# Seven block products instead of eight for three pieces of the first down projection

## What is computed

```python
def swiglu(h, w_gate, w_up, w_down):                     # first block, inner width 2816
    return (jax.nn.silu(h @ w_gate) * (h @ w_up)) @ w_down
...
x = x + swiglu(rmsnorm(x, norm_ffn), w_ffn_gate, w_ffn_up, w_ffn_down)
return rmsnorm(x, norm_final)                             # and then the second block's norm
...
h = h + jnp.square(jax.nn.relu(u @ w_ff1)) @ w_ff2        # second block, inner width 4096
```

## Time and profile before

| | |
|---|---|
| time, median of 3 runs | 928.12 us (928.05 to 928.24) |
| time of the profiled execution | 928.59 us |
| its span in the trace | 926.8 us |
| TensorE busy (PE) | 912.8 us, 98% |
| VectorE busy (DVE) | 661.6 us, 71% |
| ScalarE busy (ACT) | 500.9 us, 54% |
| GpSimd busy (POOL) | 90.1 us, 10% |
| mean granted TensorE clock | 0.998 |

### The profile page before, as it was taken

The page is one execution under the profiler, slowest core; times in us unless marked ns, Lnnn a source line. Parts: engine busy times, 40 slices in busy tenths (PEclk is TensorE's granted clock), DMA queues, the critical chain, the costliest instruction groups (busy, mean ns, idle before and its releaser), DMA issues.

```text
span 926.8 us, 15782 instructions
## 1 busy us (share of the span) xinstructions
PE 912.8 (98%) x6399; PEld 782.2 (84%) x6399; DVE 661.6 (71%) x1075; ACT 500.9 (54%) x786; POOL 90.1 (10%) x103
## 2 busy tenths in 40 slices
PE   9999999999999999999999999999999999999998
PEld 8999987787778788888888889988988788888886
DVE  5786446556777768777744769578867578888886
ACT  5654345556864456555544674546436455565551
POOL 1000000131004200000000000003350003330000
PEclk9999999999999999999999999999999999999999
DMA  9769842244446435555543442231000445455631
GB/s 326 300 131 275 320 182 91 92 182 136 182 195 252 184 114 204 199 199 195 184 182 119 182 162 92 91 105 80 3 2 21 164 182 182 182 192 197 226 112 46
DMA packets 16872, 149.80 MB, mean 162 GB/s; under 512 B 1744, under 2 KB 6224, under 8 KB 8352
## 3 DMA queue, kind: packets, MB, share of 16 engines
q1 hardware_dynamic: 14688, 140.24, 40.9%
q0 software_dynamic: 1296, 5.24, 3.2%
q10 hardware_dynamic: 816, 3.31, 0.9%
HBM read 144.59 MB, written 4.19 MB: 161 GB/s over the span
## 4 chain that ended last, share of the span: by engine, by line
PE 89%; DVE 4%; ACT 3%; issue 2%; POOL 1%; DMA 0%; ACTq 0%; DVEq 0%; POOLq 0%
PE bank L743 46%; PE bank L785 15%; PE bank L787 7%; PE bank L700 4%; PE bank L1577 3%; PE bank L950 1%; POOL HN L3382 1%; PE bank L987 1%; PE bank L1024 1%; DVE W_LOW L2423 1%; PE bank L861 1%; ACT W_HIGH L1811 1%; PE bank L1444 1%; DMA PRM<-params_dram 0%; PE bank L1338 0%
## 5 line engine op out<-in xcount | busy, mean ns | idle before, releaser
L2423 DVE TENSOR_TENSOR W_LOW<-weights,W_HIGH 128x2048 fp32r<-128x2048 f32 (+1 forms) x98 | 222.4, 2270 | 106.5 <-ACT W_HIGH L1811 105.4
L1811 ACT ACTIVATE W_HIGH<-weights 128x2048 fp32r<-128x2048 f32 (+1 forms) x98 | 184.0, 1878 | 138.4 <-PE bank L743 137.2
L785 PE MATMUL bank<-OVER_BOTH,W_HIGH 128*128 128x512 f32 x608 | 211.6, 392 | 0.2 <-DVE W_LOW L2423 0.2
L787 PE MATMUL bank<-OVER_BOTH,W_LOW 128*128 128x256 f32 x608 | 170.0, 280 | 0.0
L785 PEld LDWEIGHTS bank<-OVER_BOTH,W_HIGH 128*128 128x128 f32 x608 | 114.1, 188 | 25.9 <-DVE W_LOW L2423 0.5
L787 PEld LDWEIGHTS bank<-OVER_BOTH,W_LOW 128*128 128x128 f32 x608 | 114.2, 188 | 0.0
L1749 ACT ACTIVATE ARENA<-bank 128x256 f32<-128x256 f32 x76 | 29.1, 384 | 84.0 <-PE bank L787 83.2
L743 PE MATMUL bank<-W_HIGH,HID_HIGH 128*128 128x512 f32 x164 | 64.0, 390 | 0.0
L743 PE MATMUL bank<-W_HIGH,HID_LOW 128*128 128x512 f32 x164 | 63.9, 390 | 0.0
L743 PE MATMUL bank<-W_LOW,HID_HIGH 128*128 128x512 f32 x164 | 63.9, 390 | 0.0
L743 PE MATMUL bank<-FIRST_HIGH,W_HIGH 128*128 128x256 f32 x216 | 61.5, 285 | 0.0
(11 more groups left out here) (577 smaller groups left out, 1956.2 us busy)
## 6 DMA issues: line engine op xcount, KB each, us to landing
weights<-weights_dram SPq DMA_DIRECT2D x62, 2048.0 KB, 7.9
weights<-weights_dram SPq DMA_DIRECT2D x3, 1024.0 KB, 9.3
bias_rows_dram<-ARENA POOLq DMA_DIRECT2D x1, 3072.0 KB, 39.4
BIAS<-params_dram ACTq DMA_DIRECT2D x1, 1997.0 KB, 14.0
weights<-weights_dram SPq DMA_DIRECT2D x1, 1664.0 KB, 6.5
weights<-weights_dram SPq DMA_DIRECT2D x1, 1584.0 KB, 8.1
weights<-weights_dram SPq DMA_DIRECT2D x3, 512.0 KB, 5.8
X<-x_dram ACTq DMA_DIRECT2D x2, 512.0 KB, 4.2
```

The source lines that it names most:

```text
L785: pe.matmul(o[:, :].rearrange("p (q n) -> p q n", q=2), high, OVER_BOTH[:, :, k, :], start=(k == 0), stop=False, skip_group_check=True)
L787: ins = pe.matmul(o[:, 0:S], low, OVER_HT[:, k, :], start=False, stop=(k == KD - 1), skip_group_check=True)
L1811: act.activation(part_of(like_source(piece_parts(k)[0], k), k), part_of(piece_source(k), k), ACT.Copy)\
L2423: dve.tensor_tensor(low, part_of(src, k), high.bitcast(F32), ALU.subtract)\
```

## The change

Three things are changed. (1) `SEVEN` gets the pieces 2, 4 and 6 of `down1`: they are computed with seven products, with the same operations around them as in `down2`. GpSimd's sums of hidden blocks and their splits lie in the first hidden layer (`ffn1`). (2) The extra banks of `down1` are added to X by a function `extras` in two steps that stand in VectorE's program inside the loop over the pieces: step 0 behind the split of piece 8 (the ninth), step 1 behind the split of piece 9 (the tenth). ScalarE's copy of bank 0 stands behind its split of piece 8. In `down2` both steps stay behind all splits. (3) TensorE waits for `x_gained` before the keep-running matmuls after `down1`, since these write banks 0 to 3.

```diff
-SEVEN = (2, 4, 6, 8, 10, 12)
+SEVEN = [("down1", c) for c in (2, 4, 6)] + [("down2", c) for c in (2, 4, 6, 8, 10, 12)]
...
-        W_SUMS_AT = [0, 0, 1, 0, 1, 0]
+        W_SUMS_AT = [0, 0, 1, 0, 0, 2, 0, 2, 0]
...
         def wait_sums_place(eng, n):
-            if n == 0:
-                eng.wait_ge(sem("jobs_written"), len(JOBS))
-            elif n == W_SUMS_AT.index(1):
-                eng.wait_ge(sem("down2_pieces_read"), 4)
+            kind = SEVEN[n][0]
+            before = [SEVEN[m][1] for m in range(n) if SEVEN[m][0] == kind and W_SUMS_AT[m] == W_SUMS_AT[n]]
+            if before:
+                eng.wait_ge(sem(kind + "_pieces_read"), before[-1] + 1)
+            elif W_SUMS_AT[n]:
+                eng.wait_ge(sem(kind + "_pieces_read"), 4)
             else:
-                last = max(m for m in range(n) if W_SUMS_AT[m] == W_SUMS_AT[n])
-                eng.wait_ge(sem("down2_pieces_read"), SEVEN[last] + 1)
+                eng.wait_ge(sem("jobs_written"), max(k for job, k in JOB_AT.items() if job[0] == "ffn" + kind[-1]) + 1)
...
                 for c in range(nk // 2 - 2):
-                    if kind == "down2" and c in SEVEN:
+                    if (kind, c) in SEVEN:
                         ready(2 * c + 1)
-                        ins = seven_products(c, high, low)
+                        ins = seven_products(kind, c, high, low)
...
+            pe.wait_ge(sem("x_gained"), 1)
             norm_transposes(2, (4, 3, 2))
...
             def hidden1_high(c):
+                if ("down1", c - 1) in SEVEN:
+                    hidden_sums_high(SEVEN.index(("down1", c - 1)))
                 act.wait_ge(sem("hidden_ready"), c + 1)
...
-            for k in range(PIECE_AT["down1", 0, 0] + 2, in2 + 1):
+            down1 = PIECE_AT["down1", 0, 0]
+            for k in range(down1 + 2, in2 + 1):
                 split_high(k)
+                if k == down1 + last_of("down1") + 2:
+                    act.wait_ge(sem("down1_pieces_read"), last_of("down1") + 1)
+                    act.activation(EXTRA1[:, 0, :], BK[0][:, :], ACT.Copy).then_inc(sem("cross_by_act"), 1)
...
+            def extras(kind, sums, scales, copied, step):
+
+                def gain(tt, dc, src):
+                    xs = X[:, tt, dc * 512:(dc + 1) * 512]
+                    return dve.scalar_tensor_tensor(out=xs, in0=src, scalar=scales[:, tt:tt + 1], in1=xs, op0=ALU.mult, op1=ALU.add)
+
+                if step == 0:
+                    dve.wait_ge(sem(kind + "_pieces_read"), last_of(kind) + 1)
+                    dve.wait_ge(sem("cross_by_act"), copied)
+                    link(dve.tensor_tensor(sums[:, 1, :], BK[2][:, :], sums[:, 0, :], ALU.add))
+                    gain(0, 0, sums[:, 0, :])
+                    link(gain(0, 1, sums[:, 1, :]))
+                    link(dve.tensor_tensor(sums[:, 0, :], BK[3][:, :], sums[:, 1, :], ALU.add))
+                else:
+                    gain(0, 1, BK[1][:, :])
+                    gain(1, 0, sums[:, 0, :])
+                    link(gain(1, 1, sums[:, 0, :]))
+                    link(gain(1, 1, BK[1][:, :]))
...
             def hidden1_low(c):
+                if ("down1", c - 1) in SEVEN:
+                    hidden_sums_low(SEVEN.index(("down1", c - 1)))
                 hidden_low(HID1_HIGH, HID1_LOW, slice(2 * c, 2 * c + 2), HF1[:, c % 2, :], c)
...
                 if c >= 2 and t == 0:
                     dve.wait_ge(sem("hidden_split" if j else "hidden_ready"), c - 1)
+                    if j and ("down1", c - 2) in SEVEN:
+                        dve.wait_ge(sem("hidden_sums"), 3 * SEVEN.index(("down1", c - 2)) + 3)
...
-            for k in range(PIECE_AT["down1", 0, 0] + 2, in2 + 1):
+            down1 = PIECE_AT["down1", 0, 0]
+            for k in range(down1 + 2, in2 + 1):
                 split_low(k)
+                if k - down1 - last_of("down1") in (2, 3):
+                    extras("down1", EXTRA1, HALF_RSTD, 4 * FF1_CHUNKS + 1, k - down1 - last_of("down1") - 2)
```

More of the change, by code:

```diff
@@ L493, in seven @@
             kind, i, j = PIECES[k]
-            return SEVEN.index(2 * i + j) if kind == "down2" and 2 * i + j in SEVEN else None
+            return SEVEN.index((kind, 2 * i + j)) if (kind, 2 * i + j) in SEVEN else None
         def part_of(t, k):
@@ L1115, in _, with seven_products @@
                 branch_product(i)
[L1118 to L1122, removed]
+            def seven_products(kind, c, high, low):
+                n = SEVEN.index((kind, c))
+                w, hid, sums = split_piece(kind, c // 2, c % 2), HID_SUMS[n], W_SUMS[W_SUMS_AT[n]]
+                opens, closes = n == first_of(kind), c == last_of(kind)
+                if opens:
                     for b in range(4):
-                        pe.wait_ge(sem(f"job_out{b}"), len(range(b, len(JOBS), 4)))
+                        pe.wait_ge(sem(f"job_out{b}"), len(range(b, state["job"], 4)))
                 def product(o, left, right, own):
                     return product3(o[:, :], [[part] for part in left], [[part] for part in right],
-                                    first=own and n == 0, last=own and n == len(SEVEN) - 1)
+                                    first=own and opens, last=own and closes)
                 def hidden(t, k):
@@ L2352, in _ @@
             act.wait_ge(sem("hidden_split"), FF1_CHUNKS + FF2_KT // 2)
-            act.wait_ge(sem("down2_pieces_read"), SEVEN[-1] + 1)
+            act.wait_ge(sem("down2_pieces_read"), last_of("down2") + 1)
             act.activation(HF2[:, 0, :], BK[0][:, :], ACT.Copy).then_inc(sem("cross_by_act"), 1)
@@ L3272, in _ @@
             link(dve.reciprocal(RSTD, SUMSQ))
[L3274 to L3278, removed]
             def hidden2_low(q):
-                if q - 1 in SEVEN:
-                    hidden_sums_low(SEVEN.index(q - 1))
+                if ("down2", q - 1) in SEVEN:
+                    hidden_sums_low(SEVEN.index(("down2", q - 1)))
                 hidden_low(HID2_HIGH, HID2_LOW, slice(2 * q, 2 * q + 2), HF2[:, q % 2, :], FF1_CHUNKS + q)
@@ L3304, in _ @@
                 split_low(k)
-            def gain(tt, dc, src):
-                xs = X[:, tt, dc * 512:(dc + 1) * 512]
-                return dve.scalar_tensor_tensor(out=xs, in0=src, scalar=RSTD[:, tt:tt + 1], in1=xs, op0=ALU.mult, op1=ALU.add)
-            dve.wait_ge(sem("down2_pieces_read"), SEVEN[-1] + 1)
-            dve.wait_ge(sem("cross_by_act"), 4 * (FF1_CHUNKS + FF2_CHUNKS) + 1)
-            link(dve.tensor_tensor(HF2[:, 1, :], BK[2][:, :], HF2[:, 0, :], ALU.add))
-            gain(0, 0, HF2[:, 0, :])
-            link(gain(0, 1, HF2[:, 1, :]))
-            link(dve.tensor_tensor(HF2[:, 0, :], BK[3][:, :], HF2[:, 1, :], ALU.add))
-            gain(0, 1, BK[1][:, :])
-            gain(1, 0, HF2[:, 0, :])
-            link(gain(1, 1, HF2[:, 0, :]))
-            link(gain(1, 1, BK[1][:, :]))
+            extras("down2", HF2, RSTD, 4 * (FF1_CHUNKS + FF2_CHUNKS) + 2, 0)
+            extras("down2", HF2, RSTD, 4 * (FF1_CHUNKS + FF2_CHUNKS) + 2, 1)
             for b in range(3):
@@ L3382, in _, with hidden_sums @@
                     pool.tensor_tensor(mix, mix, TMP[:, n % 2, :], ALU.add).then_inc(sem("mixed_by_pool"), 1)
+            def hidden_sums(n):
+                kind, q = SEVEN[n]
+                pool.wait_ge(sem("hidden_ready"), (FF1_CHUNKS if kind == "down2" else 0) + q + 1)
+                low, hidden = HID_RAW[n], HF2 if kind == "down2" else HF1
+                a = [[hidden[:, q % 2, (1 - k) * S + t * P:(1 - k) * S + (t + 1) * P] for k in range(2)] for t in range(2)]
+                pool.tensor_tensor(low[:, 2, :], a[0][0], a[1][0], ALU.subtract)
+                pool.tensor_tensor(low[:, 0, :], a[1][0], a[1][1], ALU.add).then_inc(sem("hidden_sums"), 1)
+                pool.wait_ge(sem("hidden_sums"), 3 * n + 1)
+                pool.tensor_tensor(low[:, 1, :], low[:, 0, :], a[0][0], ALU.subtract).then_inc(sem("hidden_sums"), 1)
+                pool.wait_ge(sem("hidden_sums"), 3 * n + 2)
+                pool.tensor_tensor(low[:, 3, :], a[0][1], low[:, 1, :], ALU.subtract).then_inc(sem("hidden_sums"), 1)
+            for n in range(first_of("down2")):
+                hidden_sums(n)
             wait_fill_out(pool, ("key_T",))
@@ L3446, in _ @@
                 masks("gd", lv)
-            for n, q in enumerate(SEVEN):
-                pool.wait_ge(sem("hidden_ready"), FF1_CHUNKS + q + 1)
-                low = HID_RAW[n]
-                a = [[HF2[:, q % 2, (1 - k) * S + t * P:(1 - k) * S + (t + 1) * P] for k in range(2)] for t in range(2)]
-                pool.tensor_tensor(low[:, 2, :], a[0][0], a[1][0], ALU.subtract)
-                pool.tensor_tensor(low[:, 0, :], a[1][0], a[1][1], ALU.add).then_inc(sem("hidden_sums"), 1)
-                pool.wait_ge(sem("hidden_sums"), 3 * n + 1)
-                pool.tensor_tensor(low[:, 1, :], low[:, 0, :], a[0][0], ALU.subtract).then_inc(sem("hidden_sums"), 1)
```

(4 more changed lines are left out.)

38 lines of the change are left out of this document (25 added, 13 removed).

## The result

| kernel | device us | executions | ratio to before (95%) |
|---|---|---|---|
| before | 928.11 median (927.94 to 928.48) | 8 | 1 |
| changed | 930.57 median (929.13 to 931.69) | 8 | 1.0025 [1.0016, 1.0034] |

The change costs 2.46 us: slower, by a little more than a measurement of this kernel can tell from no change. The forecast was 929.3 us, 1.3 us less, with a range of its own from 928.8 to 929.8, which the result leaves; the wide range holds it because that one was drawn up to 931.1 us for the rivals A and C. A change slower by more than a measurement can tell had been given 0.18. The profiled execution took 930.74 us (span 928.9), against 928.59 (span 926.8) before, so 2.15 us have to be found in the trace.

What follows compares the result with a forecast made beforehand. TensorE, busy 98% of the span, was taken as the bound. Step 1's 2.90 us less the 1.74 us saved gave 1.16 us, so 928.12 + 1.16 = 929.3 us; own range 928.8 to 929.8, wide range 928.2 to 931.1.

Steps and rivals of the forecast that it cites:

- the wide range: Whole kernel: the eight-times-in-ten range, 928.2 to 931.1 us.
- rival A: `down1`, around piece 10: the clock falls in TensorE's wait, costing 1.7 us more, 931.0 us; chance 0.10.
- C: First hidden layer: VectorE's added operations lose their cover, 1.8 us more, 931.1 us; chance 0.04.
- The saving: `down1`: three pieces losing three matmuls each save 1.74 us by the end of piece 7, at most 2.04.
- Sums, step 0, `x_gained`: First hidden layer and `down1`: sums, first group of extra operations (0.35 us to spare) and new TensorE wait cost nothing.
- The wait: `down1`, load for piece 10: TensorE's wait grows from 0.22 to 3.12 us, so piece 10 starts 1.16 us later.
- The clock: `down1`, around the wait: dense 512-column matmuls on both sides, so no clock fall was added to the 1.16 us.
- the sum: Whole kernel: a net 1.16 us later, without a clock fall, giving a median of 929.3 us; chance 0.65.

Runs made afterwards that it cites:

- (7): The changed kernel without the eight operations that add the extra banks of `down1` to X: 926.11 us, ratio 0.9977.
- experiment 1: The changed kernel with step 1's four operations behind the split of piece 10 instead of ahead of it: 927.44 us, ratio 0.9994.
- experiment 6: The changed kernel with two of step 1's operations ahead of piece 10's split and two behind it: 927.79 us, ratio 0.9997.
- experiment 2: The changed kernel with twelve idle 512-column matmuls in TensorE's wait for piece 10: 929.37 us, ratio 1.0013.
- (8): The kernel before with two added VectorE operations between the splits of pieces 9 and 10: 929.68 us, ratio 1.0016.
- experiment 10: The kernel before with four added VectorE operations between the splits of pieces 9 and 10, and twelve idle matmuls in TensorE's wait: 931.24 us, ratio 1.0030.
- experiment 4: The kernel before with four added VectorE operations, results unused, between the splits of pieces 9 and 10: 933.65 us, ratio 1.0050.
- experiment 5: The changed kernel with step 1 behind piece 10's split, and LATENT's low split made by GpSimd instead of VectorE: 930.90 us, ratio 1.0034.
- experiment 9: The changed kernel with step 1 behind piece 10's split, and VectorE splitting LATENT behind the additions of the banks: 926.61 us, ratio 0.9982.
- experiment 3: The changed kernel with seven products for pieces 2 and 4 of `down1` only, extra operations behind splits 6 and 7: 926.96 us, ratio 0.9987.

## Why the prediction was right or wrong

The stage lengths put every step side by side (us; wait of the load for piece 10; clock in the profiled execution):

| kernel | stage | wait | clock behind it |
|---|---|---|---|
| before | 59.88 | 0.22 | full |
| no extra operations (7) | 58.09 | 0.22 | full |
| second group later (1) | 58.09 | 0.29 | full |
| half of the group (6) | 59.48 | 1.61 | full |
| group ahead, matmuls in the wait (2) | 60.98 | filled | full |
| changed | 62.60 | 3.18 | half for 3.4 us |
| before, two operations (8) | 61.45 | 1.79 | full |
| before, four, matmuls in the wait (10) | 63.05 | filled | full |
| before, four operations (4) | 64.62 | 3.37 | half for 3.5 us |

*The saving.* Right: 1.74 forecast; 1.83 at ScalarE's marks, 1.79 in the stage without extra operations.

*Sums, step 0, `x_gained`.* Right to take nothing: the stage's first matmul came at 461.86 (461.92 before); piece 9's split waits for ScalarE as usual (0.47 us at 505.88, forecast 505.96), so step 0 is hidden; and the distance to the next stage stays 5.98 us.

*The wait.* Right in place, cause and size: forecast 3.12 us and a net loss of 1.16, measured 3.18, and 1.10 with the clock held up (experiment 2). Experiments 1, 6 and 7 make the wait disappear or halve by the place or number of the operations alone, and experiments 4 and 8 make it without the change.

*The clock.* This is the step that failed. The sum stayed at 1.16 because "TensorE runs 512-column matmuls without a pause up to the wait and after it". Both halves of that are true in the trace, and the clock fell all the same: rival A, which I gave 0.10. Its size was right: 1.7 us taken from another fall in the earlier trace rows, 1.62 measured. Experiments 2 and 10 show that it is the standing still: with the same wait for VectorE's result and TensorE kept at work, the clock stays up behind it in the profile and the 1.6 us are gone. That the time lies in the wide range is rival A's doing, not the sum's. The Trainium skill, "TensorE: Matmul & The Clock Gate", section "Why this matters for your kernels", asks that TensorE not be left idle for long between bursts. I had let the dense work on both sides weigh more than that rule; the changed kernel's profile agrees with the rule, with the 0.50 at 514.5 to 517.9.

*How often.* Seven of eight executions of the changed kernel took 930.53 us or more, with a mean clock of 0.994 to 0.998, the eighth 929.13 with 0.998, near the sum without a fall. Only the first was profiled; that the seven share its cause is argued from their times, not shown. Experiment 4 says that the fall doesn't come every time: four of its executions took 933.54 us or more, with a mean clock of 0.994 to 0.996, the fifth took 930.87 with 0.999. That lies among the times of experiment 10 (930.53 to 932.44), where TensorE was kept at work, so the wait was there and the loss behind it by all appearances not. The fifth wasn't profiled.

*Why the median is not rival A's 931.0.* In the profiled pair the later stretch gave back 0.55 us, because the fall of the earlier trace rows didn't come. I had counted it in both. That fall wasn't cheaper for TensorE than the one in `down1`. The same matmuls at that place, before and after:

```profile
670.56 2.82 PE L1517 MATMUL bank<-ARENA 64*64 64x128 f32 x48
673.18 1.92 PE L1620 MATMUL bank<-ARENA 64*64 64x64 f32 x24
```

```profile
673.13 1.53 PE L1531 MATMUL bank<-ARENA 64*64 64x128 f32 x48
674.50 1.56 PE L1634 MATMUL bank<-ARENA 64*64 64x64 f32 x24
...
682.47 0.68 PE L1591 MATMUL bank<-ARENA 64*64 64x64 f32 x16 [0.97 <-issue]
```

The two groups took 1.6 us longer at the lower clock, as much as the fall among 512-column matmuls cost (1.62). But at full clock TensorE comes so early to the place at 682.47 that it waits 0.97 us there, a wait that the kernel before doesn't have, and with it most of the gain goes. It is also what raised `L1591 <- issue` from 1.4 us in three waits to 2.3 in four. So a fall of 3.4 us costs its 1.6 us in either place, and what reaches the end depends on the waits behind it: all of it in `down1`, 0.55 us here.

*Open.* Time without a matmul, and the clock behind it, in the profiles: 1.19 us (experiment 6), 1.37 (8) and 2.46 (1, between the stages) without a fall; 2.76 (changed), 2.94 (4) and 4.27 (5) with one. With one profiled execution of each, and the fifth of experiment 4, these rows are no threshold. Nor do they say what decides whether the clock falls in the stretch of the earlier trace rows: it did before and in experiment 4, but in none of the ten other profiles.

## What to carry to other kernels

Before work is put in front of a helper's hand-over, look for the smallest wait that the fed engine already shows at exactly that place: 0.22 us on one load told that four operations would cost their whole length there, though they are free one or two splits earlier. A wait of some 3 us on TensorE (3.18) can cost half as much again (1.62) through the clock behind it, even amid dense matmuls, so a stall is priced with and without that. A saving or a fall somewhere counts only as far as the next wait of the same engine lets it through (0.55 of 1.6 us). And moving the work isn't done when the wait is gone: follow the helper to its next hand-over, where experiment 1 lost 1.43 us again, and change the order there too (experiment 9) or take less (experiment 3).

## What the hardware showed that I had not expected

- TensorE's clock fell some 1.2 us behind the end of a 2.8 us pause, not in it, and stayed at half level for 3.4 us (0.50 in the row at 514.5) while 512-column matmuls ran without a pause. In experiment 4 it fell almost with the pause's end (load at 515.27, half level from 515.4), in experiment 5 0.4 us behind it.
- While one GpSimd operation ran (128x2048, two inputs, 511.49 to 516.11), a pair of VectorE's operations with two inputs in SBUF (the memory that holds every tile but the banks) took 5.41 us instead of 1.41, so 4.0 of the 4.2 us that they lay beside it were lost; the one that reads a bank, begun 0.25 us before it, took its usual 0.75. The Trainium skill, "GPSIMD Engine Reference", section "1. Specifications", says that GpSimd shares its interfaces to SBUF with VectorE and that they contend when VectorE has two inputs there; experiment 5 agrees, with those numbers. It is one kernel: a second form of the operation wasn't tried. GpSimd's sums of hidden blocks in the changed kernel, all of one size, point to the other direction, but no experiment took them apart. In the first hidden layer the first of a group stands beside a split of VectorE and takes 2.59 us, the last 0.46; in the second hidden layer it is the third that stands beside such a split (782.63, 2.38 us), and the first takes 0.46:

```profile
375.56 2.59 POOL L3423 TENSOR_TENSOR ARENA<-ARENA 128x128 f32<-128x128 f32 x1 [66.45 <-DVE ARENA L2854]
...
379.71 0.46 POOL L3428 TENSOR_TENSOR ARENA<-ARENA 128x128 f32<-128x128 f32 x1
...
781.67 0.46 POOL L3423 TENSOR_TENSOR BIAS<-ARENA 128x128 f32<-128x128 f32 x1 [6.70 <-DVE ARENA L3341]
...
782.63 2.38 POOL L3426 TENSOR_TENSOR BIAS<-BIAS,ARENA 128x128 f32<-128x128 f32 x1
```

```profile
375.53 2.29 DVE L2443 TENSOR_TENSOR W_LOW<-weights,W_HIGH 128x2048 fp32r<-128x2048 f32 x1
...
782.24 2.46 DVE L2443 TENSOR_TENSOR W_LOW<-weights,W_HIGH 128x2048 fp32r<-128x2048 f32 x1 [0.65 <-ACT W_HIGH L1825]
```
